# Starting every on-chip buffer behind the two weight tile buffers 64 bytes further on

## What is computed

```
x = x + hybrid_mixer(rms_norm(x), ...)      # 1024 x 7440 input projection, SSD and attention branches, three 1024 x 1024 projections
x = x + hier_moe(rms_norm(x), ...)          # 4 groups x 8 experts, 2 experts per token; gate, up, down matrices of 1024 x 256
x = x + sigmoid(rms_norm(x) @ w_ple_gate) * (p @ w_ple)
x = rms_norm(x)
h = rms_norm_2(x) ; proj = h @ w_in_2       # 1024 x 5280 input projection
u_hy   = long convolutions through FFT spectra, gated, @ w_hy_out
u_attn = 8-head bidirectional attention with low-rank q and kv, gated, @ w_attn_out
x = x + (gate_hy * u_hy + gate_attn * u_attn) @ w_out
```

## Time and profile before

| what | value |
|---|---|
| median of three runs | 787.89 us |
| the profiled execution's own time | 787.62 us |
| its span in the trace | 785.8 us |
| mean granted share of TensorE's clock | 0.976 |
| TensorE matmul busy | 727.4 us, 93% |
| TensorE weight load busy | 544.3 us, 69% |
| VectorE busy | 476.6 us, 61% |
| ScalarE busy | 328.0 us, 42% |
| moved by DMA | 190.00 MB |

### The profile page before, as it was taken

How to read it: one execution, slowest core, us unless ns; L and a number is a source line. 1 busy time by engine, 2 the same in 40 slices (tenths; PEclk the granted TensorE clock), 3 DMA queues, 4 the chain that set the end, 5 groups by cost and what they waited for, 6 DMA issues and landing times.

```text
span 785.8 us, 11043 instructions
## 1 busy us (share of the span) xinstructions
PE 727.4 (93%) x4596; PEld 544.3 (69%) x4596; DVE 476.6 (61%) x886; ACT 328.0 (42%) x488; POOL 17.9 (2%) x15
## 2 busy tenths in 40 slices
PE   7999999999999999976799798678999999999998
PEld 7988886778878886543245254346899968687686
DVE  5898868766656647332242131128776699887763
ACT  6565447646364415110110110127664553366630
POOL 0000000000000000000000000001010003000000
PEclk9999999999999999997889899899999999999999
DMA  9765543234368679899999999996454563453311
GB/s 316 237 237 167 160 158 111 103 120 149 107 224 319 261 318 421 299 366 421 422 420 402 421 420 422 418 399 228 121 191 158 189 213 112 133 184 108 108 53 54
DMA packets 63157, 190.00 MB, mean 242 GB/s; under 512 B 7482, under 2 KB 11836, under 8 KB 51133
## 3 DMA queue, kind: packets, MB, share of 16 engines
q1 hardware_dynamic: 61326, 184.44, 63.3%
q10 hardware_dynamic: 1774, 4.79, 1.8%
HBM read 188.16 MB, written 1.05 MB: 241 GB/s over the span
## 4 chain that ended last, share of the span: by engine, by line
PE 73%; DMA 16%; DVE 6%; ACT 2%; issue 1%; POOL 0%; SPq 0%; DVEq 0%; ACTq 0%
PE pb L518 69%; DMA WHo<-in_w_exp_up 8%; DMA raw<-in_w_exp_up 6%; PE pb L527 4%; DMA WHo<-in_w_exp_down 2%; DVE rawo L1805 1%; ACT arena L1312 1%; DMA c<-in_cst 1%; ACT WH L1284 0%; DVE arenao L1839 0%; DVE arena L1859 0%; POOL small L2734 0%; SPq L2781 0%; DVE arena L2122 0%; DVE HDl L1839 0%
## 5 line engine op out<-in xcount | busy, mean ns | idle before, releaser
L1284 ACT ACTIVATE WH<-raw 128x2048 fp32r<-128x2048 f32 (+5 forms) x80 | 145.3, 1825 | 83.7 <-PE pb L518 70.2
L1805 DVE TENSOR_TENSOR rawo<-raw,WH 128x2048 fp32r<-128x2048 f32 (+5 forms) x80 | 172.4, 2172 | 3.8 <-ACT WH L1284 3.8
L518 PE MATMUL pb<-WH,HTh 128*128 128x512 f32 (+2 forms) x352 | 142.0, 403 | 3.0 <-ACT arena L1312 1.4
L518 PE MATMUL pb<-rawo,HTh 128*128 128x512 f32 (+2 forms) x352 | 135.1, 384 | 0.0
L518 PE MATMUL pb<-WH,HTl 128*128 128x512 f32 (+2 forms) x352 | 135.0, 384 | 0.0
L518 PEld LDWEIGHTS pb<-WH,HTh 128*128 128x128 f32 x352 | 66.2, 188 | 20.4 <-issue 6.6
L518 PEld LDWEIGHTS pb<-rawo,HTh 128*128 128x128 f32 x352 | 66.2, 188 | 13.1
L518 PEld LDWEIGHTS pb<-WH,HTl 128*128 128x128 f32 x352 | 66.4, 189 | 11.5 <-issue 0.7
L518 PE MATMUL pb<-WH,arenao 128*128 128x512 f32 x224 | 69.7, 392 | 2.4 <-ACT arena L1312 1.2
L2360 DVE TENSOR_TENSOR rt_<-rt_,pb 128x256 f32<-128x256 f32 x8 | 3.4, 421 | 95.0 <-ACT rt_ L1571 95.0
L518 PE MATMUL pb<-raw,arena 128*32 128x256 f32 (+1 forms) x256 | 49.3, 487 | 11.7 <-DMA raw<-in_w_exp_up 6.3
(11 more groups left out here) (370 smaller groups left out, 1272.3 us busy)
## 6 DMA issues: line engine op xcount, KB each, us to landing
raw<-in_w_in SPq DMA_DIRECT2D x46, 1024.0 KB, 5.2
raw<-in_w_exp_up SPq DMA_DIRECT2D x18, 1024.0 KB, 21.3
arena<-in_w_exp_gate SPq DMA_DIRECT2D x13, 1024.0 KB, 23.5
arena<-in_w_exp_down SPq DMA_DIRECT2D x12, 1024.0 KB, 16.9
WHo<-in_w_exp_down SPq DMA_DIRECT2D x9, 1024.0 KB, 23.3
raw<-in_w_out SPq DMA_DIRECT2D x8, 1024.0 KB, 5.4
raw<-in_w_exp_gate SPq DMA_DIRECT2D x8, 1024.0 KB, 17.5
WHo<-in_w_exp_up SPq DMA_DIRECT2D x8, 1024.0 KB, 22.7
```

Source lines behind the costliest of these rows:

```text
L518: return e.matmul(o, l, r, start=start, stop=stop, skip_group_check=True)
L1284: e.activation(h_, r_, ACT.Copy).then_inc(hi.sem, hi.mark(k))
L1805: e.tensor_tensor(l_, r_, h_.bitcast(F32), ALU.subtract).then_inc(lo.sem, lo.mark(k))
```

## The change

A buffer `stagger` of 16 float32, 64 bytes in each partition, is allocated behind `raw`. Nothing reads or writes it. Every buffer behind it starts 64 bytes later: `HDh` at 83136, `arena` at 93376, `HTh` at 185536 and so on. `WH` and `raw` stay where they are. The same is done in the second list of names by which these buffers are reached with the other type. All engines' instructions, their order, sizes and waits are as before.

```diff
 SLOT = 2048
+STAGGER = 16
 SCRATCH = 1024
...
-        shared = (("WH", [128, NSPLIT, SLOT], F32R), ("raw", [128, NRAW, SLOT], F32), ("HDh", [128, 1280], F32R),
+        shared = (("WH", [128, NSPLIT, SLOT], F32R), ("raw", [128, NRAW, SLOT], F32), ("stagger", [128, STAGGER], F32), ("HDh", [128, 1280], F32R),
                   ("HDl", [128, 1280], F32R), ("arena", [128, 18944], F32), ("cv_", [128, 1024], F32),
                   ("sg_", [128, 1024], F32), ("XN", [128, 2, D], F32), ("HTh", [128, 8, L], F32R), ("HTl", [128, 8, L], F32R))
         with ExitStack() as other:
-            WHf, raw_r, HDhf, HDlf, arena_r, cv_r, sg_r, XN_r, *HTf = (
+            WHf, raw_r, _, HDhf, HDlf, arena_r, cv_r, sg_r, XN_r, *HTf = (
                 other.enter_context(nc.sbuf_tensor(n + "o", shape, F32 if dt is F32R else F32R))
                 for n, shape, dt in shared)
-        WH, raw, HDh, HDl, arena, cv_, sg_, XN, *HT = (sb(n, shape, dt) for n, shape, dt in shared)
+        WH, raw, _, HDh, HDl, arena, cv_, sg_, XN, *HT = (sb(n, shape, dt) for n, shape, dt in shared)
```

## The result

The changed kernel took 792.34 us (median of five runs, 790.81 to 792.74) against 787.34 us of the kernel before, run beside it (786.55 to 787.90). The ratio is 1.0065, 95% interval 1.0049 to 1.0081. It is slower by 5 us; 9 us of gain were forecast.

What follows compares the result with a forecast made beforehand. TensorE was taken to bound the dense stages, DMA the expert stage. A 10.4 us gain on activation-stationary matmuls, less 1.0 us swallowed by waits, all else 0, gave 778.5 us; likeliest range 776 to 781, 8-in-10 range 773 to 784.

Steps and rivals of the forecast that it cites:

- What bounds the kernel: TensorE's rate sets the time up to 297 us and from 530 us on; DMA does from 334 to 530 us.
- That 64 bytes of distance matter at all: Against the skill's rule: 64 bytes between stationary and moving operand, modulo 256, change matmul spacing, by 6.7 ns in `cx` rows.
- The mechanism that I had drawn: A matmul's stream and the next stationary operand's load disturb each other when aligned modulo 256; 64 bytes remove half of 13.4 ns.
- Step 1: 1548 activation-stationary matmuls in `gemm_chunk`, D from 0 to 64: 6.7 ns less each, 10.4 us; bounds nothing and 20.7 us.
- Step 2: 648 weight-stationary matmuls (`channels` and its kin), D from 0 to 192: taken as 0, at most 4.3 us off.
- The size of 6.7 ns itself: Gain per matmul at D = 64, read from 113.3 against 120 ns in `cx` chunks 1 and 5.
- Steps 3 to 5: Matmuls with both operands behind `raw`, splits, expert matmuls, DMA into shifted buffers: each taken as 0; DMA upper bound 11.3 us.
- The first one: Rival: the good sign depends on which operand is which, so dense matmuls gain 0 to 2 ns: 783.5 to 787.9, chance 0.12.
- The one that ended slower: Rival: shifted rows slow the expert stage's DMA stream; 789.8 us, or 799 if matmuls gain nothing; chance 0.04.

Runs made afterwards that it cites:

- e1: The changed kernel with the unused buffer 256 bytes long instead of 64: 787.48 us, ratio 0.9999 to the kernel before.
- e2: The changed kernel with the 64 unused bytes ahead of `WH` instead of behind `raw`, so all buffers move together: 787.37 us, ratio 1.0002 to the kernel before.
- e7: The changed kernel with the 64 unused bytes behind `arena` instead of behind `raw`: 789.81 us, ratio 1.0030 to the kernel before.
- e11: The kernel before with 64 unused bytes between `HTh` and `HTl`: 788.70 us, ratio 1.0016 to the kernel before.
- e6: The changed kernel with each 512-column matmul of `gemm_chunk` cut into two of 256: 793.15 us; the kernel before with the same cut took 804.18 us.
- e10: The kernel before with its six `cx` tiles 64 bytes further on in their slots and 256 bytes more behind `WH`: 786.97 us, ratio 0.9989.
- e3: The changed kernel with the unused buffer 192 bytes long instead of 64: 787.37 us, ratio 1.0001 to the kernel before.
- e8: The changed kernel with the unused buffer 32 bytes long instead of 64: 791.25 us, ratio 1.0054 to the kernel before.

## Why the prediction was wrong

**What bounds the kernel.** Right: the two dense stages follow TensorE's matmul distance. In the first stage the distances of its 864 matmuls of 512 columns (227.9 to 233.3 ns) and 264 of 256 (119.3 to 117.5) add up to 4.2 us more, and 4.1 are measured; in the second they add up to 1.3 us more, of which 0.6 reach the end; where the rest went was not followed. The expert stage stayed DMA-bound and started 4 us later.

**That 64 bytes of distance matter at all.** Right: `e1`, `e2` and `e7` show distances of 228 and 233 ns by the place of the operands alone. The rule of the Trainium skill that the two read ports are independent ("TensorE: Matmul & The Clock Gate", section "Part 2: What happens when you issue a matmul") does not cover it. The mechanism that I had drawn, a stream disturbed by the load of the next operand and relieved by 64 bytes, is not borne out: `e11` speaks against that pair, and at 512 columns 64 bytes add to the time. What collides, and why the width turns the sign, stays open.

**Step 1, the term that failed.** "I take 6.7, since the amount on top is the same at 256 and 512 columns." The rows with D = 64 had 256 columns. The 13.5 ns on top are equal at both widths at D = 0 only. At D = 64 they become 20 ns at 512 columns (233.2 - 213.3) and 9 to 11 at 256 (115.9 - 106.7 in `e6`, 117.8 - 106.7 in `e10`). The 1416 matmuls of 512 columns did not give 6.7 ns each but cost 5.0, 7.1 us instead of -9.5. The 48 of 288 columns showed nothing, as the earlier trace rows had it for D = 128, and the 84 of 384 cost some 2 ns. A warning was in reach: at 288 columns the rows gave no gain at D = 128, while chunk 2 of the `cx` tile, with 256 columns at the same D, takes 704 ns for its six matmuls against 717 at D = 0, by the start times in the trace before. A response that differs between 256 and 288 columns should not be carried to 512.

**Step 2.** The 648 matmuls with weights stationary gave 2.7 ns each, 1.7 us, where 0 was taken and 4.3 was the bound. The rows in hundredths of a microsecond hid it: chunks 3 and 4 both read 0.71 us, but the trace before has 705 and 717 ns, 2 ns for each matmul. Together 7.1 + 0.2 - 1.7 = 5.6 us by the distances, measured 5.0.

**The size of 6.7 ns itself** was read from the third `cx` tile, whose groups of 128, 128 and 16 columns alternate. With 128-column loads alone the same D gave 117.8 ns in the first two `cx` tiles (`e10`), not 113. Off D = 0 the spacing at 256 columns holds at about 113 or about 118 ns (`e3`, `e6`), and which of the two depends on what came before: behind the third tile's 16-column loads it was 113. So even at 256 columns the rows read overstated what D = 64 gives in an ordinary tile, 2 to 4 ns and not 6.7.

**Steps 3 to 5.** Right as far as the runs can tell. The splits kept their durations. DMA into shifted buffers cost nothing beyond the 1.3 us of the interval, with `e2` as the test: all tiles moved, 787.37 us. That the expert matmuls' changes were hidden fits the sum, but the expert stage varies by 3 us from trace to trace, more than the 2.6 us that were at stake.

**The rivals.** The first one, that the sign is bound to the operands' roles, came nearest in kind, but roles are not what decides. The one that ended slower had the wrong mechanism: the DMA rate was 412 GB/s, against 411 before. That width could turn the sign was in none of them, and both bounds of step 1 were gains of nothing or more, so that no case in the sum let TensorE become slower. A gain that was read at one shape needed, for the other shape, a bound on the side of a loss.

## What to carry to other kernels

In this kernel, whose dense stages are back-to-back fp32r matmuls with a load for each, the place of the two operands modulo 256 bytes is worth 2% of a matmul of 512 columns and up to 3% of one of 256: aligned operands were best at 512 moving columns, and every displacement tried was better at 256. Moving buffers by 32 or 64 bytes, as an added small buffer does unasked, cost the whole kernel half a percent (`e8`, and the change itself); a pad to 256 bytes undid it (`e1`). Other types and kernels were not measured. A difference found between two rows holds for their shape; before it is carried to another width, look for a row of that width or keep both signs in the range.

## What the runs showed that I had not expected

- At 512 columns, 32 bytes of distance act as fully as 64 or 224 (233.1, 233.2 and 233.2 ns); 192 is nearly harmless (229.8).
- The effect changes sign with the width of the stream: two matmuls of 256 columns at D = 64 take 2 x 115.9 = 232 ns, about what one of 512 takes there (233), while at D = 0 they take 240 against 228.
- In the three matmuls of a product in `e11` the extra time sits on the one whose own stationary operand is displaced.
- At 256 columns the same D gave 118 or 113 ns according to what had run before (`e10`, chunks 0 and 4).
